# Reading a kernel's input in a second, feature-major layout instead of turning it on TensorE

## The chip, the cores and the metric

The kernel runs on one core of one Trainium2 chip. The metric is the device time of one execution in microseconds (us). The core has five engines that run side by side and meet only at semaphores: TensorE (PE; its weight loads are shown as PEld), VectorE (DVE), ScalarE (ACT), GpSimd (POOL) and SyncE (SP), which here issues all the transfers between the chip's memory (HBM) and the on-chip memory (SBUF). TensorE writes to eight banks of PSUM, 128 partitions of 512 float32 numbers each.

## The reference, cut to what matters

Two model blocks run one after the other over 256 tokens of 1024 features, in float32. The change touches the very first step of the first block: the norm of the input and its product with `w_in`.

```python
def rms_norm(x, g):
    y = xf * lax.rsqrt(jnp.mean(xf * xf, axis=-1, keepdims=True) + EPS)
    return (y * g.astype(jnp.float32)).astype(x.dtype)
...
h = rms_norm(x, norm_mix[l])
z = jnp.einsum('bsd,de->bse', h, w_in[l])
a_x, a_y, b_q, b_f, b_i, b_g, c_q, c_k, c_v = jnp.split(z, split_at, axis=-1)
```

The parts of `z` feed a gated recurrence with a short convolution, a gated linear attention and a softmax attention; then follow an output product, a feed-forward pair, and the second block with its table of experts.

## The kernel before

**Tiles of weights.** Nearly all weights come as a stream of 128x1024 float32 tiles (512 KB each, 432 in all), tile n into slot n mod 4 of `raw`. Each is split into two parts for TensorE: ScalarE copies it rounded into `whi` (function `hi`, line 526, one ACTIVATE), then GpSimd computes the rest `wlo = raw - whi` (function `lo`, line 448, one TENSOR_TENSOR that reads two tensors of SBUF). SyncE may load tile n once `lo` is done with tile n-4; `hi` of tile n also waits until TensorE has used tile n-4. A product of a tile is three matmuls for each 128x128 piece: high by high, low by high, high by low.

**The input.** The activations are split in the same way into `xh` and `xl`, with features on the partitions and the 256 tokens in the free dimension, eight pieces k = 0 to 7 of 128x256. Before, x arrives with tokens on the partitions (`xres`, two transfers, one for each half of the features). TensorE turns it with 16 transposes (line 1066) into banks 0 to 3, two pieces k in each bank, as float32. ScalarE reads a bank and writes `xh` (function `upper`, line 570, gain of the norm as scale). VectorE reads the bank again and writes `xl = bank * gain - xh` (function `turned`, line 1516). TensorE's first tile (`f_tile`, lines 922 to 924) waits for `turned_lo` before every second k. The row of inverse roots of the norm is applied later, when a product is read out of its bank (`in_f`, line 1591): ScalarE sums the squares of x (`sums`, line 545), GpSimd takes the inverse root (`root`, lines 467 and 469), TensorE lays it out as a row in the middle of tile 1 (`mix_row`, line 1117), VectorE copies it to `mix_r` (line 1583).

**The order at the start.** SyncE issues: tile 0, x first half, the identity matrix `ident`, the columns of gains and biases `col`, x second half, tiles 1 to 3, five transfers of constants (all counted by one semaphore, `consts1_in`), then tile 4 and on. ScalarE: `hi(0)`, four pieces of `xh`, `hi(1)`, four pieces of `xh`, two sums of squares, `hi(2)`, `hi(3)`, then two loads of activation tables with a small ACTIVATE after each, `hi(4)` and on. GpSimd: `lo(0)`, `lo(1)`, `root`, `lo(2)`, `lo(3)` and on. TensorE: matmuls on a constant tile (`warm_up`, line 1055), the transposes, then eight tiles with their products in banks 4 and 5 in turn, the small block products of `lru_gates` (line 1077) behind tile 4. Then follows the group `in_M` (lines 964 to 966), in which a tile fills four banks, and between its tiles the scores of the linear attention (line 1108).

Every engine runs its own list in the order in which it is written; a wait holds back all that stands behind it on that engine. TensorE waits for a tile's low part with the first of these lines, and in tile 0 for a pair of pieces of `xl` with the second:

```python
pe.wait_ge(lo_done, count)
pe.wait_ge(S("turned_lo"), turn(turned, 4, k // 2 + 1))
```

Of the kernel before, what the change touches and what calls it, by code (L numbers as in the profile page):

```python
# [53 lines left out]
def acc_freed(group, bank):  # L54
# [4 lines left out]
    if group == "in_M":  # L59
        return (("turned_lo", turn("mix", 4, 1)), ("gy_done", 1), ("ri_done", 1), ("ld_done", 1))[bank]  # L60
# [18 lines left out]
def acc_filled(group, bank):  # L79


    before = GROUPS[:GROUPS.index(group)]
    n = sum(4 if g in TRANSPOSES else 3 for g in before) + bank + 1
    if group == "wout" and bank == 2:
        return n + 2
    return n - 1 if group == "mlp_T" and bank < 2 else n
# [14 lines left out]
F_ORDER = [0, 1, 2, 3, 6, 7, 4, 5, 8, 12, 9, 13, 10, 14, 11, 15]  # L101
Y_BANKS = [0, 1, 4, 5]
# [51 lines left out]
def build(nc, x, stream, ada, cols, rows, lru_w, hgmask, causal, alibi, iota, walr, wup, sguw, keys, out):  # L154
    ctx = ExitStack()
    with ctx:
# [177 lines left out]
        def _(sp):  # L334
# [11 lines left out]
            for n in range(1, R):  # L346
                tile(n, n * P, None)
            sp.dma_start(lw.rearrange("p a b -> p (a b)"), lru_w).then_inc(S("consts1_in"), 16)
            sp.dma_start(msk.rearrange("p a b -> p (a b)").bitcast(U32), hgmask).then_inc(S("consts1_in"), 16)
            sp.dma_start(tmp, rows[:, 0:D].to_broadcast([P, D])).then_inc(S("consts1_in"), 16)  # L350
            sp.dma_start(ali, alibi).then_inc(S("consts1_in"), 16)

            sp.dma_start(gate1, rows[:, 5 * D:6 * D].to_broadcast([P, D])).then_inc(S("gate1_b"), 16)
# [10 lines left out]
            for n in range(R, T_FFN):  # L364
                tile(n % R, n * P, n - R + 1)
                if n in range(T_IN_M, T_IN_M + R):
# [78 lines left out]
        def _(pool):  # L445
# [75 lines left out]
        def _(act):  # L521
# [63 lines left out]

            hi(0, 0, None)
            act.wait_ge(S("col_in"), 16)
            upper("mix_T", c_("mix"), banks=(0, 1))
            hi(1, 0, None)
            upper("mix_T", c_("mix"), banks=(2, 3))  # L590
# [1724 lines left out]
```

## Time and profile before

| | us |
|---|---|
| device time, median of 3 runs | 1384.27 |
| lowest and highest of them | 1382.73, 1386.12 |
| profiled execution, first to last instruction (span) | 1383.7 |
| median of the runs less that span | 0.6 |
| TensorE busy in the span | 1354.1 |
| VectorE, ScalarE, GpSimd busy | 788.2, 713.0, 1056.8 |

The profile is of one execution; the page states its span and no other time of it. How to read it: the timeline lists an engine's instructions in order of time with the start, the duration and, in square brackets, how long the engine sat idle before and what released it. Matmuls overlap, so their durations are longer than the distance between their starts; it is the starts that tell the pace. "PEclk", the granted clock, is 1.00 at TensorE's upper level (2.4 GHz) and 0.50 at the lower (1.2 GHz); in the first microseconds it reads 1.00 although the rows of the warm-up show the slower pace.

### The profile page before, as it was taken

The numbers are of one execution on the slowest core, as the hardware profiler recorded it, in microseconds if no ns is written. First come the engines' busy times: TensorE is split into PE (matmuls) and PEld (weight loads), VectorE is DVE, ScalarE is ACT, GpSimd is POOL, SyncE is SP. The second block draws the span as 40 slices with busy tenths as digits, with TensorE's granted clock in tenths as the row PEclk, the third lists the DMA queues.
The fourth block names the chain that finished last, engine by engine and source line by source line (L and its number), as shares of the span: only waits on it lengthen the run. The fifth ranks groups of instructions, "written<-read, shape, count | busy, mean of one in ns | idle before, by whom it ended". The sixth has DMA issues, their size and how long they took to land.

```text
span 1383.7 us, 27404 instructions
## 1 busy us (share of the span) xinstructions
PE 1354.1 (98%) x9123; PEld 1178.4 (85%) x9123; DVE 788.2 (57%) x1616; ACT 713.0 (52%) x1139; POOL 1056.8 (76%) x466
## 2 busy tenths in 40 slices
PE   8999999999998999999999999999999999999997
PEld 8788999998776887899999988888788888888886
DVE  4755433336159327269990388888877878411113
ACT  7355655555364444435556544444455555566564
POOL 6655788886777786868888877777667777888885
PEclk9999999999999999999999999999999999999999
DMA  8444777774644456745555544454444445565552
GB/s 315 170 169 165 249 282 284 279 257 142 214 148 156 141 178 259 243 138 184 181 183 181 177 164 167 167 167 164 168 140 167 168 166 168 187 236 197 192 189 105
DMA packets 73057, 263.10 MB, mean 190 GB/s; under 512 B 8224, under 2 KB 9120, under 8 KB 72624
## 3 DMA queue, kind: packets, MB, share of 16 engines
q1 hardware_dynamic: 73008, 262.46, 55.0%
q8 instruction: 29, 0.48, 0.1%
q14 instruction: 20, 0.16, 0.0%
HBM read 259.81 MB, written 2.62 MB: 190 GB/s over the span
## 4 chain that ended last, share of the span: by engine, by line
PE 90%; DVE 5%; ACT 2%; issue 1%; DMA 1%; POOL 1%; SPq 0%; POOLq 0%; ACTq 0%; DVEq 0%
PE bank L964 14%; PE bank L965 14%; PE bank L966 14%; PE bank L945 10%; PE bank L922 8%; PE bank L924 8%; PE bank L923 8%; PE bank L946 5%; PE bank L1436 3%; PE bank L949 1%; DVE arena L1956 1%; PE bank L948 1%; PE bank L1108 1%; POOL wlo L448 1%; PE bank L1418 1%
## 5 line engine op out<-in xcount | busy, mean ns | idle before, releaser
L448 POOL TENSOR_TENSOR wlo<-raw,whi 128x1024 fp32r<-128x1024 f32 x432 | 1043.0, 2426 | 293.8 <-ACT whi L526 292.5
L526 ACT ACTIVATE whi<-raw 128x1024 fp32r<-128x1024 f32 x432 | 455.5, 1057 | 337.3 <-PE bank L966 254.2
L964 PE MATMUL bank<-whi,xhl 128*128 128x512 f32 x800 | 320.3, 400 | 12.7 <-DVE arena L1929 5.6
L966 PE MATMUL bank<-whi,xhl 128*128 128x512 f32 x800 | 313.9, 392 | 0.0
L965 PE MATMUL bank<-wlo,xhl 128*128 128x512 f32 x800 | 313.6, 392 | 0.0
L922 PE MATMUL bank<-xhl,whi 128*128 128x256 f32 x896 | 255.0, 285 | 1.9 <-DVE xhl L1516 1.1
L923 PE MATMUL bank<-xhl,whi 128*128 128x256 f32 x896 | 253.5, 283 | 0.0
L924 PE MATMUL bank<-xhl,wlo 128*128 128x256 f32 x896 | 253.4, 283 | 0.0
L945 PE MATMUL bank<-xhl,whi 128*128 128x512 f32 x616 | 222.0, 399 | 1.0 <-DVE xhl L1511 1.0
L964 PEld LDWEIGHTS bank<-whi,xhl 128*128 128x128 f32 x800 | 151.5, 189 | 48.7 <-issue 6.7
L966 PEld LDWEIGHTS bank<-whi,xhl 128*128 128x128 f32 x800 | 151.5, 189 | 32.8
L965 PEld LDWEIGHTS bank<-wlo,xhl 128*128 128x128 f32 x800 | 151.7, 190 | 29.7
L922 PEld LDWEIGHTS bank<-xhl,whi 128*128 128x128 f32 x896 | 171.7, 192 | 5.0 <-DVE xhl L1516 1.3
L923 PEld LDWEIGHTS bank<-xhl,whi 128*128 128x128 f32 x896 | 171.8, 192 | 1.2
L946 PE MATMUL bank<-xhl,wlo 128*128 128x256 f32 x616 | 171.9, 279 | 0.0
L924 PEld LDWEIGHTS bank<-xhl,wlo 128*128 128x128 f32 x896 | 171.7, 192 | 0.0
L2158 DVE TENSOR_TENSOR xhl<-bank,xhl 128x256 fp32r<-128x256 f32 x128 | 53.8, 420 | 148.5 <-ACT bank L878 148.4
L851 ACT ACTIVATE arena<-bank 128x256 f32 x128 | 49.2, 384 | 172.8 <-DVE bank L2168 119.0
L945 PEld LDWEIGHTS bank<-xhl,whi 128*128 128x128 f32 x616 | 115.6, 188 | 25.2 <-DVE xhl L1511 1.3
L2143 DVE TENSOR_TENSOR xs<-bank,xs 128x768 bf16<-128x768 f32 x128 | 121.7, 951 | 0.0
L946 PEld LDWEIGHTS bank<-xhl,wlo 128*128 128x128 f32 x616 | 116.1, 189 | 2.6 <-issue 0.2
L2139 DVE TENSOR_TENSOR bank<-xs,bank 128x256 f32<-128x256 f32 (+1 forms) x128 | 54.4, 425 | 55.2 <-PE bank L1436 53.8
(321 smaller groups left out, 1511.0 us busy)
## 6 DMA issues: line engine op xcount, KB each, us to landing
raw<-stream SPq DMA_DIRECT2D x432, 512.0 KB, 3.3
arena<-ada SPq DMA_DIRECT2D x48, 512.0 KB, 4.9
arena<-rows SPq DMA_DIRECT2D x5, 512.0 KB, 7.6
xs<-x SPq DMA_DIRECT2D x2, 512.0 KB, 6.5
arena<-rows SPq DMA_DIRECT2D x1, 1024.0 KB, 5.7
x_spill<-xs SPq DMA_DIRECT2D x1, 1024.0 KB, 6.3
xs<-x_spill SPq DMA_DIRECT2D x1, 1024.0 KB, 5.5
arena<-hgmask SPq DMA_DIRECT2D x1, 512.0 KB, 8.3
```

The lines of the kernel that those rows point to most:

```text
L448: nc.gpsimd.tensor_tensor(wlo[:, slot, :], raw[:, slot, :], whi[:, slot, :].bitcast(F32), ALU.subtract).then_inc(lo_done, 1)
L526: nc.scalar.activation(whi[:, slot, :], raw[:, slot, :], ACT.Copy).then_inc(hi_done, 1)
L922: nc.tensor.matmul(dst, h_, xh[:, k, :], start=(k == 0), stop=False)
L923: nc.tensor.matmul(dst, h_, xl[:, k, :], start=False, stop=False)
L924: last = nc.tensor.matmul(dst, l_, xh[:, k, :], start=False, stop=(k == KC - 1))
L945: nc.tensor.matmul(dst, h_, xhl[:, :, k, :], start=(k == 0), stop=False)
L946: nc.tensor.matmul(dst[:, 0:T], l_, xh[:, k, :], start=False, stop=False)
L964: nc.tensor.matmul(bank[b][:, :], ah[:, ts], whi[:, slot, cs], start=start, stop=False)
L965: nc.tensor.matmul(bank[b][:, :], ah[:, ts], wlo[:, slot, cs], start=False, stop=False)
L966: last = nc.tensor.matmul(bank[b][:, :], al[:, ts], whi[:, slot, cs], start=False, stop=final)
L2139: ttt(same, bc(0, HALF), counts[:, :, HALF * half:HALF * (half + 1)].to_broadcast([P, 4, HALF]), ALU.is_equal).then_inc(S("same"), 1)
L2143: ttt(oneA[:, slot], same.unsqueeze(1).to_broadcast([P, 3, 4, HALF]), picks[:, 2:5, ts].unsqueeze(3).to_broadcast([P, 3, 4, HALF]), ALU.mu ...
```

## The change

The host hands over x twice: as before (tokens on the partitions, now as two transfers of one token half each), and as `xT`, with features on the partitions, in the layout that `xh` and `xl` have. `xT` is loaded in two halves of 512 KB into the buffer `xg`, which is otherwise used later. ScalarE and VectorE split it from there, so both read SBUF where they read a bank of PSUM. The 16 transposes are gone; four warm-up matmuls that stood between them now stand at the start, 20 in all. The order of the first transfers is new, four of the constants move behind tiles 4, 5 and 6, and `lru_w` gets a semaphore of its own. ScalarE takes `hi(2)` ahead of the sums of squares; GpSimd takes `lo(2)` ahead of `root`. The products of the first tiles go to banks 4, 5, 0, 2, 4, 5, 4, 5; `mix_row` moves from the middle of tile 1 to that of tile 2, and `lru_gates` from behind tile 4 to behind tile 5.

```diff
+F_BANKS = [4, 5, 0, 2, 4, 5, 4, 5]
...
+            xT_all = xg.rearrange("p a b -> p (a b)")
             tile(0, 0, None)
-            x_halves = x.rearrange("p (a d) -> p a d", a=TT)
-            sp.dma_start(xres[:, :, 0:512], x_halves[:, :, 0:512]).then_inc(S("x_in0"), 16)
+            sp.dma_start(col[:, :], cols).then_inc(S("col_in"), 16)
+            x_turned(0)
+            tile(1, P, None)
+            x_turned(1)
+            tile(2, 2 * P, None)
+            x_part(0)
+            x_part(1)
+            tile(3, 3 * P, None)
             sp.dma_start(ident[:, :], iota[:, P:2 * P]).then_inc(S("ident_in"), 16)
-            sp.dma_start(col[:, :], cols).then_inc(S("col_in"), 16)
-            sp.dma_start(xres[:, :, 512:1024], x_halves[:, :, 512:1024]).then_inc(S("x_in1"), 16)
...
-            for n in range(2):
+            for n in range(3):
                 lo(n, n + 1)
             root(S("squares"), squared("mix"), s_(SS["mix"]), rs("mix"), 1.0 / D)
-            for n in range(2, R):
-                lo(n, n + 1)
+            lo(3, R)
...
+            def x_upper(half):
+                act.wait_ge(S(f"xT_in{half}"), 16)
+                for k in range(4 * half, 4 * half + 4):
+                    last = nc.scalar.activation(xh[:, k, :], xg[:, k, :], ACT.Copy, scale=c_("mix", k))
+                    if k % 2:
+                        last.then_inc(S("turned_hi"), 1)
...
-            warm_up(16)
-            pe.wait_ge(S("ident_in"), 16)
-            for b in range(4):
-                if b == 2:
-                    warm_up(4)
-                pe.wait_ge(S(f"x_in{b // 2}"), 16)
-                for tt in range(TT):
-                    for j in range(2):
-                        k = 2 * b + j
-                        last = nc.tensor.transpose(bank[b][:, j * T + tt * P:j * T + (tt + 1) * P],
-                                                   xres[:, tt, k * P:(k + 1) * P], ident[:, :])
-                last.then_inc(acc_ready, 1)
+            warm_up(20)
...
-                if n >= 2:
-                    pe.wait_ge(S("in_f"), n - 1)
-                if n == 1:
+                if n >= R:
+                    pe.wait_ge(S("in_f"), n - 3 if n < 6 else n - 1)
+                if n == 2:
...
-                if n == 4:
+                if n == 5:
                     lru_gates()
...
-            turned("mix", c_("mix"))
+            for b in range(4):
+                v.wait_ge(S("turned_hi"), b + 1)
+                for k in (2 * b, 2 * b + 1):
+                    last = stt(xl[:, k, :], xg[:, k, :], c_("mix", k), xh[:, k, :].bitcast(F32), ALU.mult, ALU.subtract)
+                last.then_inc(S("turned_lo"), 1)
```

SyncE's list from the start of the program, before (the names are the destination and the source of a transfer; `xs` is the buffer of x, `arena` a large buffer in which `xg`, the constants and much else lie):

```order
L338 DMA raw<-stream 128x1024
L342 DMA xs<-x 128x2x512
L343 DMA ident<-iota 128x128
L344 DMA col<-cols 128x108
L345 DMA xs<-x 128x2x512
L338 DMA raw<-stream 128x1024 x3
L348 DMA arena<-lru_w 128x256
L349 DMA arena<-hgmask 128x1024
L350 DMA arena<-rows 128x1024
```

and in the changed kernel:

```order
L339 DMA raw<-stream 128x1024
L349 DMA col<-cols 128x108
L342 DMA arena<-xT 128x1024
L339 DMA raw<-stream 128x1024
L342 DMA arena<-xT 128x1024
L339 DMA raw<-stream 128x1024
L345 DMA xs<-x 128x1024 x2
L339 DMA raw<-stream 128x1024
L357 DMA ident<-iota 128x128
L358 DMA arena<-lru_w 128x256
L339 DMA raw<-stream 128x1024
```

One small transfer instead of two stands ahead of the input, tile 1 stands between the input's halves, and 1 MB more is loaded.

ScalarE's list from its first tile on, before (`whi` is a tile's high part, `xhl` holds `xh` and `xl`):

```order
L526 ACTIVATE whi<-raw 128x1024
L570 ACTIVATE xhl<-bank,col 128x256 x4
L526 ACTIVATE whi<-raw 128x1024
L570 ACTIVATE xhl<-bank,col 128x256 x4
L545 ACTIVATE arena,st<-xs 128x1024 x2
L526 ACTIVATE whi<-raw 128x1024 x2
```

and in the changed kernel:

```order
L537 ACTIVATE whi<-raw 128x1024
L600 ACTIVATE xhl<-arena,col 128x256 x4
L537 ACTIVATE whi<-raw 128x1024
L600 ACTIVATE xhl<-arena,col 128x256 x4
L537 ACTIVATE whi<-raw 128x1024
L556 ACTIVATE arena,st<-xs 128x1024 x2
L537 ACTIVATE whi<-raw 128x1024
```

The source of the eight pieces is now in SBUF, and tile 2's high part has passed the sums of squares.

## Rows read from the trace of the kernel before

**Rows 1.** The page: busy us, share of the span, number of instructions of each engine.
```profile
PE 1354.1 (98%) x9123; PEld 1178.4 (85%) x9123; DVE 788.2 (57%) x1616; ACT 713.0 (52%) x1139; POOL 1056.8 (76%) x466
```

**Rows 2.** Timeline, TensorE, 0 to 19 us; last row: all its waits from 18.9 to 72.5.
```profile
1.06 5.83 PE L1055 MATMUL bank<-arena 128*128 128x128 f32 x32 [1.06 <-POOL arena L473]
...
10.74 0.36 PE L922 MATMUL bank<-xhl,whi 128*128 128x256 f32 x1
...
13.54 0.39 PE L922 MATMUL bank<-xhl,whi 128*128 128x256 f32 x1 [1.13 <-DVE xhl L1516]
...
16.46 0.28 PE L924 MATMUL bank<-xhl,wlo 128*128 128x256 f32 x1
...
18.95 0.35 PE L922 MATMUL bank<-xhl,whi 128*128 128x256 f32 x1 [0.57 <-DVE arena L1591]
...
PE bank L922 <- DVE arena L1591: 0.6, 1, 0.6
```

**Rows 3.** Timeline, SyncE's first issue of x, and both transfers' time to landing.
```profile
1.18 0.66 SPq L342 DMA_DIRECT2D xs<-x  x1
...
DMA to landing us min/median/max: 6.5/6.5/6.6
```

**Rows 4.** Timeline, ScalarE, 0 to 19 us.
```profile
4.08 1.06 ACT L526 ACTIVATE whi<-raw 128x1024 fp32r<-128x1024 f32 x1 [2.07 <-DMA raw<-stream]
8.76 1.57 ACT L570 ACTIVATE xhl<-bank,col 128x256 fp32r<-128x256 f32 x4 [3.63 <-PE bank L1066]
10.79 1.06 ACT L526 ACTIVATE whi<-raw 128x1024 fp32r<-128x1024 f32 x1 [0.46 <-DMA raw<-stream]
...
13.18 1.07 ACT L545 ACTIVATE arena<-xs 128x1024 f32<-128x1024 f32 x1
...
17.29 1.28 ACT L597 ACT_TABLE_LOAD   x1
```

**Rows 5.** Timeline, GpSimd, 5 to 22 us.
```profile
5.28 2.35 POOL L448 TENSOR_TENSOR wlo<-raw,whi 128x1024 fp32r<-128x1024 f32 x1 [4.28 <-ACT whi L526]
11.93 2.38 POOL L448 TENSOR_TENSOR wlo<-raw,whi 128x1024 fp32r<-128x1024 f32 x1 [4.30 <-ACT whi L526]
...
15.74 0.71 POOL L469 TENSOR_TENSOR st<-st 128x2 f32<-128x2 f32 x1
16.42 4.75 POOL L448 TENSOR_TENSOR wlo<-raw,whi 128x1024 fp32r<-128x1024 f32 x2
```

**Rows 6.** Timeline, VectorE, second half of `xl`.
```profile
12.61 1.66 DVE L1516 SCALAR_TENSOR_TENSOR xhl<-bank,col,xhl 128x256 fp32r<-128x256 f32 x4 [1.23 <-ACT xhl L570]
```

**Rows 7.** Timeline, VectorE and GpSimd, 392 to 418 us; last row: L2067 from 655.5 to 656.
```profile
392.44 3.40 DVE L1948 SCALAR_TENSOR_TENSOR arena<-arena,st 128x1024 f32<-128x1024 f32 x1 [2.38 <-POOL st L469]
...
416.59 1.22 DVE L1952 SCALAR_TENSOR_TENSOR arena<-arena 128x1024 f32<-128x1024 f32 x1 [10.74 <-ACT arena L794]
...
392.37 15.73 POOL L448 TENSOR_TENSOR wlo<-raw,whi 128x1024 fp32r<-128x1024 f32 x5
...
L2067 DVE TENSOR_TENSOR arena<-arena x1: 2622/2622/2622, 655.1 to 655.1; 128x256 f32<-128x256 f32 x1
```

**Rows 8.** Timeline, TensorE; then stretches: busy by engine, granted clock, DMA share, GB/s.
```profile
439.61 0.77 PE L964 MATMUL bank<-whi,xhl 128*128 128x512 f32 x1 [5.59 <-DVE arena L1929]
...
441.02 0.63 PE L964 MATMUL bank<-whi,xhl 128*128 128x512 f32 x1
441.45 0.63 PE L965 MATMUL bank<-wlo,xhl 128*128 128x512 f32 x1
...
999.27 0.80 PE L964 MATMUL bank<-whi,xhl 128*128 128x512 f32 x1 [2.64 <-DVE xhl L2158]
...
438.00:439.00 1.00, 0.00 (x0) 0.00 (x0) 1.00 (x2) 0.11 (x1) 0.00 (x0) 0.89 0.54 111
...
445.00:446.00 1.00, 1.00 (x9) 1.00 (x8) 1.00 (x1) 0.90 (x1) 1.00 (x1) 0.70 0.00 0
...
998.00:999.00 1.00, 0.00 (x0) 0.00 (x0) 0.85 (x3) 0.69 (x3) 0.82 (x1) 0.78 0.29 37
```

More of the change, by code:

```diff
@@ L59, in acc_freed @@
     if group == "in_M":
-        return (("turned_lo", turn("mix", 4, 1)), ("gy_done", 1), ("ri_done", 1), ("ld_done", 1))[bank]
+        return (("in_f", 3), ("gy_done", 1), ("ri_done", 1), ("ld_done", 1))[bank]
     if group == "wout":
@@ L82, in acc_filled @@
     before = GROUPS[:GROUPS.index(group)]
-    n = sum(4 if g in TRANSPOSES else 3 for g in before) + bank + 1
+    n = sum(0 if g == "mix_T" else 4 if g in TRANSPOSES else 3 for g in before) + bank + 1
     if group == "wout" and bank == 2:
@@ L151, in sync, with build @@
         self.eng.wait_ge(self.sem, self.n)
-def build(nc, x, stream, ada, cols, rows, lru_w, hgmask, causal, alibi, iota, walr, wup, sguw, keys, out):
+def build(nc, x, xT, stream, ada, cols, rows, lru_w, hgmask, causal, alibi, iota, walr, wup, sguw, keys, out):
     ctx = ExitStack()
@@ L338, in tile, with x_turned, x_part @@
                 sp.dma_start(raw[:, slot, :], stream[bass.ds(row, P), :]).then_inc(raw_full[slot], 16)
-            tile(0, 0, None)
-            x_halves = x.rearrange("p (a d) -> p a d", a=TT)
-            sp.dma_start(xres[:, :, 0:512], x_halves[:, :, 0:512]).then_inc(S("x_in0"), 16)
-            sp.dma_start(ident[:, :], iota[:, P:2 * P]).then_inc(S("ident_in"), 16)
-            sp.dma_start(col[:, :], cols).then_inc(S("col_in"), 16)
-            sp.dma_start(xres[:, :, 512:1024], x_halves[:, :, 512:1024]).then_inc(S("x_in1"), 16)
[L346 to L353, printed above, removed]
+            def x_turned(half):
+                sp.dma_start(xT_all[:, half * D:(half + 1) * D], xT[:, half * D:(half + 1) * D]).then_inc(S(f"xT_in{half}"), 16)
+            def x_part(tt):
+                sp.dma_start(xres[:, tt, :], x[:, tt * D:(tt + 1) * D]).then_inc(S(f"x_in{tt}"), 16)
+            xT_all = xg.rearrange("p a b -> p (a b)")
+            tile(0, 0, None)
+            sp.dma_start(col[:, :], cols).then_inc(S("col_in"), 16)
[6 more added lines that the diff above has]
+            tile(3, 3 * P, None)
+            sp.dma_start(ident[:, :], iota[:, P:2 * P]).then_inc(S("ident_in"), 16)
+            sp.dma_start(lw.rearrange("p a b -> p (a b)"), lru_w).then_inc(S("lru_in"), 16)
             def ada_tile(n, row=None, free=None):
@@ L584, in upper_shifted @@
                             .then_inc(S("turned_hi"), 1)
+            def x_upper(half):
[4 more added lines that the diff above has]
+                        last.then_inc(S("turned_hi"), 1)
             hi(0, 0, None)
             act.wait_ge(S("col_in"), 16)
-            upper("mix_T", c_("mix"), banks=(0, 1))
+            x_upper(0)
             hi(1, 0, None)
-            upper("mix_T", c_("mix"), banks=(2, 3))
-            act.wait_ge(S("x_in0"), 16)
-            act.wait_ge(S("x_in1"), 16)
+            x_upper(1)
+            hi(2, 0, None)
             for tt in range(TT):
+                act.wait_ge(S(f"x_in{tt}"), 16)
                 sums(xres[:, tt, :], tt, D, xn, s_(SS["mix"]), S("squares"))
-            for n in range(2, R):
-                hi(n, 0, None)
+            hi(3, 0, None)
             nc.scalar.activation(sil, c_("c"), ACT.Sigmoid).then_inc(S("sil_sig"), 1)
@@ L1055, in warm_up @@
                     nc.tensor.matmul(bank[5][:, 0:P], ones, ones, start=True, stop=True)
[L1057 to L1068 removed]
+            warm_up(20)
             def lru_gates():
[L1071 removed]
+                pe.wait_ge(S("lru_in"), 16)
+                pe.wait_ge(S("in_f"), 4)
                 pe.wait_ge(S("xc_done"), 1)
@@ L1679, in _ @@
             totals(1)
[L1681 removed]
+            v.wait_ge(S("consts1_in"), 48)
             def level_acc(n):
```

21 lines of the change are left out of this document (14 added, 7 removed).

## The prediction

> **What bounds the kernel now.** I read the page first: TensorE is busy 1354.1 of 1383.7 us [rows 1], so only what moves TensorE counts. Then its timeline at the start. It warms up from 1.06 us, turns x from 8.00, starts tile 0 at 10.74 and idles 1.13 us in the middle of it, waiting for `xl`; it reaches tile 2 at 18.95 after 0.57 us of idle time, and from there to 72.5 us it has no other wait [rows 2]. The reader is to see that all the slack that an edit of the head can win lies before 18.95. The wait at 18.95 is printed against VectorE's `in_f`, but the code needs there only the first `in_f`, done long before, and `lo(2)`: GpSimd ran `lo(2)` and `lo(3)` from 16.42 in 4.75 us, so `lo(2)` ended at 18.8 [rows 5]. My unit is therefore the time at which TensorE begins tile 2, before 18.9. Behind it the same 6 tiles and `lru_gates` follow; only `mix_row` (about 0.25 us) moves from ahead of that point to behind it.
>
> **Transfers.** x's first half, second of the large transfers, was issued at 1.18 and landed 6.5 us later, at 7.7 [rows 3]. Tile 1, the fourth large one, landed at 10.8, where `hi(1)` started [rows 4]: 1.5 us for each 512 KB, small transfers included. In the changed order `xT` takes the second place, tile 1 the third, `xT`'s second half the fourth, tile 2 the fifth. Late bound: the places' old times, 7.9, 9.4, 10.8, 12.3. Early bound: tile 0 landed by 4.08 [rows 4], 0.4 for `col` and an estimated 1.3 for each large one: 5.7, 7.0, 8.3, 9.6. One of the two small transfers stays and the packets are longer, so I take the middle: 6.8, 8.2, 9.5, 10.9; the halves of x 12.2 and 13.5, tile 3 at 14.8. The extra 1 MB costs only this delay of x and tile 3; the moved constants have users after 25 us.
>
> **ScalarE.** Four pieces of `xh` took 1.57 us from PSUM [rows 4]; reading SBUF I take the same. Pieces 0 to 3: 6.8 to 8.4; `hi(1)` (1.06) to 9.4; pieces 4 to 7, 9.5 to 11.1; `hi(2)` to 12.2. Then the sums of squares follow x: until 14.7.
>
> **GpSimd and VectorE, the step that decides.** `lo(1)` follows `hi(1)`: 9.5 to 11.9. `lo(2)` is ready at 12.3. VectorE's `xl` falls just here, and in the changed kernel it reads `xg` and `xh`, both in SBUF. In rows 7 the same operation with two SBUF inputs took 1.22 us at 416.59, while GpSimd had nothing to run, and 3.40 us at 392.44, against `lo`: GpSimd's five `lo` took 15.73 us there in place of 12. A 128x256 operation with two SBUF inputs took 2.62 us at 655.1 [rows 7], where a piece of `xl`, the same size, takes 0.42 (1.66 for four [rows 6]). Read in order of time, the two engines take turns, a whole instruction each, and whoever comes second waits. Before the change it cost nothing: `xl` read PSUM and one SBUF tensor, and its last four pieces took 1.66 us at 12.61, in the middle of `lo(1)` from 11.93 [rows 5, 6].
>
> The Trainium skill, page "SBUF — State Buffer", section "Who interferes with whom", has this as a rule: a VectorE instruction with two SBUF inputs contends with a GpSimd instruction that reads SBUF, one with at most one SBUF input does not. By that rule, with which rows 5 to 7 agree, the sum is the one below; if the place of the inputs made no difference, it would be rival A.
>
> Pieces 0 to 3 of `xl` run from 7.8 (`lo(0)` is over at 7.63 [rows 5]) to 9.5, just before `lo(1)`. Piece 4 could start at 10.4 and waits for `lo(1)` until 11.9, done 12.3. Now `lo(2)` has come and goes first: 12.3 to 14.75. Piece 5 then ends at 15.15, pieces 6 and 7 at 16.8, since the two small instructions of `root` (0.71 us for the second [rows 5]) come between them. `lo` itself is hardly later, and nobody is queued behind it in need: tile 1 has its low part at 11.9.
>
> **TensorE.** 20 warm-ups, 40 records, end at about 7.8 (32 records took 5.83 us from 1.06 on [rows 2], 8 more at the later pace of 0.12 another 1.0). k = 0, 1 at 8.65, k = 2, 3 at 9.5 to 10.2. Then it idles until piece 5 is there, 15.15: 4.9 us. Bounds for what that does to its clock: an idle time of 1.13 us did nothing [rows 2]; one of 5.59 us, before 439.61, and one of 2.64 us, before 999.27, each ended with the granted clock at 0.50: it fell inside 438 to 439 and 998 to 999, that is 5 and 2 us after the last matmul [rows 8]. It rose again in 445 to 446, some 6 us after work had resumed at 439.61. At the lower level matmuls of 512 columns start every 0.43 us [rows 8]; in place of the 0.12 us of these (24 from 13.54 to 16.46 [rows 2]) I take 0.225. In the warm-up it must have risen sooner: 32 records in 5.83 us are, at 0.225 and 0.12 us each, 18 slow ones, an estimate of 4 us of work at the low clock [rows 2]. I take 5 us, between 4 and 6: the clock is low from before 15.15 to 20.15. Pieces 4 and 5 (6 matmuls) end at 16.5, 6 and 7 run 16.8 to 18.15, then tile 1 does 9 matmuls at the low clock and 15 in 1.8 us: tile 2 begins at 21.95.
>
> **The sum.** 21.95 + 0.25 for `mix_row` - 18.9 = +3.3 us. Removed and costed at nothing: the 16 transposes (about 2 us of TensorE) lie ahead of tile 0, where TensorE waits anyway; the gained 2 us at the first matmul (8.65 against 10.74) go into the longer wait. The four banks lift waits on `in_f`, which did not bind: `in_f(0)` comes now after `mix_row`, near 24.5, and tile 4, which needs it, at 28. `lru_gates` behind tile 5 waits for nothing new; ScalarE's `hi(9)` is queued behind it and is done with 3 us to spare. `hi(4)` waits for tile 0 (18.2) and the two table loads from 17.29 on [rows 4], as before, so `lo(4)` at about 22 is in time for tile 4. Behind tile 2 the distance to the old times stays as it is to the end. On its own execution: 1383.7 + 3.3 = 1387.0; the median stood 0.6 above the span, so 1387.6.
>
> **Rivals.**
> A. *The engines do not get in each other's way*, or tile 2 lands so late (after 12.4) that `lo(2)` lets all four pieces pass. Without any turn-taking `xl` ends at 12.1, tile 0 at 12.8, tile 1 at 15.7; then `hi(4)`, behind the table loads, holds tile 4 at 22.2 instead of 24.7: -2.5 us, 1381.8. With only `lo(1)` in the way: about -1.5. For it: the pieces are short. Against it: rows 7. This is what would make the kernel faster than before. 0.12.
> B. *Turn-taking, but the clock stays up*. Then tile 0 ends at 17.5, tile 1 at 20.4: +1.7, 1386.0. For it: 4.9 us lies below the longer of the two rows. Against it: the shorter one, 2.64 us. 0.17.
> C. *Slower than can be overlooked: xT lands at its late bound*. All of ScalarE's chain follows its landing, so 1.1 us are added, and if the clock needs 6 us rather than 5, another 0.4: +4.8, 1389.1. It decides from a landing of 7.6 us on. For it: x's first half landed at 7.7 from a like place [rows 3]. 0.14.
> D. *An early landing helps*. It does not: with `xT` at 6.0, `hi(1)` ends sooner, `lo(1)` starts before piece 3 of `xl` and blocks that one as well; `xl` ends near 16.6 all the same. It is inside the forecast.
>
> **Chances.** Forecast, turn-taking and a fallen clock: 0.52, at 1387.6. A 0.12, B 0.17, C 0.14, others 0.05 (1391 or more, or a gain that I do not see). About 0.3%, 4.1 us here, is what a measurement can tell from no change. The forecast is within it in four cases of five, B and A are within it, C is over it mostly. So faster 0.03, same 0.75, slower 0.22. The range goes from 1384.0 (under B) to 1390.0 (over C); A is left out.
>
> **What would show it.** In the changed profile: `xl` (VectorE, 128x256, eight of them) has two or three members of 2 to 3 us, beginning while `lo(1)` and `lo(2)` run; TensorE has one wait of 3 to 5 us in tile 0 behind VectorE; the granted clock is 0.50 somewhere from 13 to 20 us; tile 2 begins at 21 to 23. `xT`'s first half lands at 5.7 to 7.9. If all eight pieces take 0.4 to 0.5 us, A holds; if the wait is there and the clock reads 1.00, B. The prediction is wrong if the difference arises anywhere behind 40 us, where I expect every wait of the old profile again, shifted.

## The result, and the profile after

The changed kernel takes 1391.43 us (median of 4 runs, 1390.80 to 1393.20); the kernel before took 1383.72 beside it (4 runs). The ratio is 1.0054, with a 95% interval of 1.0041 to 1.0067. The forecast was 1387.6, range 1384.0 to 1390.0, with "slower by over 0.3%" at 0.22. The time lies above the range, and the kernel is slower. The profiled execution took 1390.8 us, with a span of 1388.5. One execution of a kernel below (a_split_warm) took 2705 us in place of some 1384 and is left out of its figures.

The head went much as forecast. Timelines of the changed kernel, 0 to 19 us: ScalarE, GpSimd, VectorE, TensorE (start, busy us, engine, line, operation, idle time ahead and what ended it):

```profile
6.96 1.70 ACT L600 ACTIVATE xhl<-arena,col 128x256 fp32r<-128x256 f32 x4 [1.68 <-DMA arena<-xT]
8.57 1.04 ACT L537 ACTIVATE whi<-raw 128x1024 fp32r<-128x1024 f32 x1
...
9.69 2.38 POOL L460 TENSOR_TENSOR wlo<-raw,whi 128x1024 fp32r<-128x1024 f32 x1 [1.92 <-ACT whi L537]
12.32 2.64 POOL L460 TENSOR_TENSOR wlo<-raw,whi 128x1024 fp32r<-128x1024 f32 x1 [0.26 <-ACT whi L537]
...
7.98 1.67 DVE L1592 SCALAR_TENSOR_TENSOR xhl<-arena,col,xhl 128x256 fp32r<-128x256 f32 x4 [7.98 <-ACT xhl L600]
10.54 5.11 DVE L1592 SCALAR_TENSOR_TENSOR xhl<-arena,col,xhl 128x256 fp32r<-128x256 f32 x4 [0.88 <-ACT xhl L600]
...
12.80 0.39 PE L939 MATMUL bank<-xhl,whi 128*128 128x256 f32 x1 [2.11 <-DVE xhl L1592]
15.70 0.58 PE L939 MATMUL bank<-xhl,whi 128*128 128x256 f32 x1 [1.92 <-DVE xhl L1592]
...
20.68 0.28 PE L939 MATMUL bank<-xhl,whi 128*128 128x256 f32 x1
```

These answer to [rows 2, 4 to 6]. The first four pieces of `xl`, with GpSimd idle, took 1.67 us; the last four, beside `lo(1)` and `lo(2)`, took 5.11, and GpSimd's second `lo` 2.64 in place of 2.35. TensorE waited twice for VectorE inside tile 0, and tile 2 begins at 20.68 (18.95 before).

TensorE's busy time and granted clock (the column behind the count) by stretch, in the head and then twice behind it, changed kernel (0.50 is the lower of the two levels, 1.2 GHz):

```profile
15.00:16.00 1.00, 0.30 (x1) 0.62 1.01 401
16.00:17.00 1.00, 1.00 (x6) 0.50 1.03 410
17.00:18.00 1.00, 1.00 (x7) 0.50 1.03 414
18.00:19.00 1.00, 1.00 (x7) 0.67 1.03 410
...
323.00:340.00 17.00, 17.00 (x90) 0.80 0.26 90
...
524.00:535.00 11.00, 9.31 (x40) 0.84 0.65 256
```

and of the kernel before:

```profile
323.00:340.00 17.00, 16.68 (x109) 1.00 0.18 63
...
524.00:535.00 11.00, 11.00 (x52) 1.00 0.60 232
```

The clock fell in the head, as forecast. It also fell at 329.3 us, for 6.8 us, and at 527.2, for 3.4: two falls that the trace of before does not have. (A fall and its length are worked out from the granted clock of stretches of 4 us: 4 us at 0.82, for instance, hold 1.44 us at the lower of the two levels; or they are read off the clock record in the trace.) The falls of [rows 8], before 439.6 and before 999.3, are there in both; the second is half as long in the changed kernel (3.4 us against 6.8).

The waits of TensorE of over 1 us from 323 to 1010 us, of the changed kernel and then of the kernel before, in us in total, times, longest:

```profile
PE bank L981 <- DVE arena L1942: 5.6, 1, 5.6
PE bank L981 <- POOL wlo L460: 2.7, 6, 0.8
PE bank L981 <- DVE xhl L2171: 2.6, 1, 2.6
PE bank L1058 <- DVE arena L2036: 1.4, 1, 1.4
PE bank L981 <- DVE xhl L1520: 1.3, 1, 1.3
```
```profile
PE bank L964 <- DVE arena L1929: 5.6, 1, 5.6
PE bank L964 <- POOL wlo L448: 2.7, 6, 0.8
PE bank L964 <- DVE xhl L2158: 2.6, 1, 2.6
PE bank L964 <- DVE xhl L1511: 1.6, 1, 1.6
```

No new wait explains a loss. The first product of the first `m_tile` (a tile of the group `in_M`) starts 1.9 us later than before; changed kernel, then before:

```profile
40.22 0.40 PE L981 MATMUL bank<-whi,xhl 128*128 128x512 f32 x1
```
```profile
38.35 0.40 PE L964 MATMUL bank<-whi,xhl 128*128 128x512 f32 x1
```

The first product behind the transposes of the second input part starts at 338.6 (333.4), +5.2. So 2 us arise in the head and 3 at one place where the program is unchanged and TensorE waits for nobody. The spans differ by 4.8 us, but that is no proof that nothing else happened: matmul by matmul the distance is +4.8 from 340 us on, +4.1 behind 446, +5.8 behind the fall at 527, +6.3 from 600 us on, and +4.8 again behind 1010, where the old kernel has the longer fall.

### The profile page after: what moved, and what is told of

Read it like the earlier page. It is cut to its first block, busy times and chain, and to the rows that moved or that the text cites. A ratio compares the mean times of both kernels' runs of the same rounds, so it can differ in the third digit from the quotient of the medians.

```text
span 1388.5 us, 27371 instructions
## 1 busy us (share of the span) xinstructions
PE 1356.2 (98%) x9107; PEld 1180.3 (85%) x9107; DVE 792.2 (57%) x1616; ACT 713.2 (51%) x1139; POOL 1057.7 (76%) x466
## 4 chain that ended last, share of the span: by engine, by line
PE 89%; DVE 5%; ACT 2%; issue 2%; DMA 1%; POOL 1%; SPq 0%; POOLq 0%; ACTq 0%; DVEq 0%
PE bank L981 14%; PE bank L983 13%; PE bank L982 13%; PE bank L962 10%; PE bank L939 8%; PE bank L941 8%; PE bank L940 8%; PE bank L963 5%; PE bank L1445 3%; PE bank L966 1%; DVE arena L1969 1%; POOL wlo L460 1%; PE bank L965 1%; PE bank L1116 1%; PE bank L1427 1%
```

## The experiments

All times are medians; "first m_tile" is the first start of line 981 or what answers to it, in the one profiled execution. The "clock" is the mean granted clock of each run's span.

| kernel | us | ratio to before (95%) | clock of the runs | first m_tile |
|---|---|---|---|---|
| before | 1383.7 to 1384.4 | | 0.992 to 0.996 | 38.3 |
| changed | 1391.43 | 1.0054 (1.0041, 1.0067) | 0.989 to 0.991 | 40.2 |
| a_repeat (the changed kernel again) | 1390.92 | 1.0046 (1.0031, 1.0061) | 0.990 to 0.992 | 42.2 |
| a_lo_waits | 1386.70 | 1.0013 (1.0002, 1.0024) | 0.990 to 0.996 | 38.4 |
| b_later | 1385.82 | 1.0010 (1.0001, 1.0018) | 0.994 to 0.996 | 39.9 |
| b_xT_bound | 1384.27 | 1.0000 (0.9991, 1.0009) | 0.993 to 0.996 | 37.5 |
| a_pad7 | 1390.38 | 1.0045 (1.0032, 1.0058) | 0.992 to 0.995 | 44.2 |
| a_pad14 | 1394.13 | 1.0079 (1.0066, 1.0091) | 0.989 to 0.992 | 44.8 |
| a_warm | 1389.23 | 1.0047 (1.0032, 1.0061) | 0.990 to 0.995 | 43.5 |
| a_split | 1384.59 | 1.0002 (0.9993, 1.0011) | 0.992 to 0.996 | 38.6 |
| a_keep | 1388.85 | 1.0035 (1.0022, 1.0047) | 0.994 to 0.995 | 43.0 |
| b_keep | 1384.40 | 1.0004 (0.9995, 1.0013) | 0.995 to 0.996 | 37.7 |
| a_split_warm | 1384.71 | 1.0003 (0.9993, 1.0013) | 0.993 to 0.996 | 37.6 |
| a_warm_one | 1388.01 | 1.0023 (1.0011, 1.0036) | 0.993 to 0.996 | 40.7 |

Names that begin with a are edits of the changed kernel, with b of the kernel before. The ratio goes over all runs of a row and is not exactly that of the two medians. Of the kernel before, 29 runs taken together had spans from 1379.0 to 1384.8, mean 1382.5; the eight of the changed kernel and its repetition lay at 1388.5 to 1390.9, mean 1389.3. The time is about 1.8 to 2.3 us above its own span in the runs of all kernels. The rows were measured at different times, each against runs of the kernel before beside it; those medians lie up to 0.7 us apart, and differences between rows carry that too. (One run of the kernel before, of 1383.49 us, reads a clock of 0.945; it is not in the range of the table.)

The questions came in this order. Is the head's loss the turn-taking and the clock, as forecast? Do the falls behind the head come from what the change moves or adds ("moved work"), from all work coming later, from luck, or from the fall in the head itself, which sets TensorE's place for what follows ("locked")? What does each part weigh?

**a_repeat**: the changed kernel without an edit.

> The changed kernel once more, for a second profile of it. Theory F (the granted clock falls at places that depend on when a stretch comes, and it comes at the same time in every execution): tile 2 begins at 20.6 us, the clock is 0.50 again from about 329 and from about 527 us, span about 1388.5 to 1391. Rival L (each execution draws its own places by luck): the falls stand elsewhere, and the span differs by 3 us or more from 1388.5. Both: 1391 us, 7 us above the kernel before.

Timelines of ScalarE, VectorE and TensorE:

```profile
8.73 1.70 ACT L600 ACTIVATE xhl<-arena,col 128x256 fp32r<-128x256 f32 x4 [3.50 <-DMA arena<-xT]
...
12.22 5.21 DVE L1592 SCALAR_TENSOR_TENSOR xhl<-arena,col,xhl 128x256 fp32r<-128x256 f32 x4 [0.79 <-ACT xhl L600]
...
16.69 0.39 PE L939 MATMUL bank<-xhl,whi 128*128 128x256 f32 x1 [4.23 <-DVE xhl L1592]
```

`xT` landed at 8.7 us here, not at 6.9; `xl` ends at 17.4, TensorE has one wait of 4.2 us, tile 2 begins at 22.6 and the first `m_tile` comes at 42.2. The clock falls again near 329 us (at 331.4, for 6.8 us), but not near 527, and the span is 1389.4. So theory F had the span and one of the two falls; rival L's span, 3 us or more away, did not come. In this and the eight later profiles that load `xT` as the change does, ScalarE starts on it between 8.2 and 9.1 us: the profile of the changed kernel is the exception.

**a_lo_waits**: GpSimd starts `lo(1)` only when `xl` is complete.

```diff
             for n in range(3):
+                if n == 1:
+                    pool.wait_ge(S("turned_lo"), 4)
                 lo(n, n + 1)
```

> The changed kernel, but GpSimd starts the low part of tile 1 only when all eight pieces of the input's low part are written, so VectorE and GpSimd never want SBUF at once there. Theory T (turn-taking costs the head its time): VectorE's last four pieces take 1.7 us instead of 5.1, TensorE's waits of 2.1 and 1.9 us in tile 0 shrink to one below 0.3, the clock stays at 1.00 up to 25 us, tile 1 begins at about 14.9 behind its own low part, tile 2 at about 17.8 instead of 20.6, so 2.8 us sooner there. Rival R (reading the second operand from SBUF is slow in itself): the last four pieces still take near 5 us and tile 2 begins later than 20.6. Of the end of the program theory T alone says nothing, since the falls of the clock further back may come or go: 1386 to 1390 us.

Timelines of VectorE and GpSimd:

```profile
11.67 1.68 DVE L1594 SCALAR_TENSOR_TENSOR xhl<-arena,col,xhl 128x256 fp32r<-128x256 f32 x4 [0.79 <-ACT xhl L602]
13.43 4.73 POOL L460 TENSOR_TENSOR wlo<-raw,whi 128x1024 fp32r<-128x1024 f32 x2 [5.76 <-ACT whi L539]
```

Apart from each other the pieces of `xl` took 1.68 us again and each `lo` 2.37. The first `m_tile` stands at 38.4, as before the change, though the clock fell in this head too (at 10.9 us, behind a wait of 3.05), which the expectation did not have; tile 2 begins at 18.8 and not at 17.8. The turn-taking is real, and most of the head's loss. Its median is still 1.0013 times before, with an interval that just excludes no change; in its profile, the slowest of its ten runs, the loss arises behind 325 us, and the clocks of its runs spread from 0.990 to 0.996.

**b_later**: the kernel before with 13 more warm-up matmuls, so that everything comes later but nothing is moved.

```diff
-            warm_up(16)
+            warm_up(29)
```

> The kernel before with 13 more warm-up matmuls at its start, nothing else: all that follows comes about 2.1 us later, as in the changed kernel behind its head. Theory F (the place in time decides where the clock falls): the clock falls near 329 us and near 527 us as in the changed kernel, the span grows by about 4.8 us, the time by 5. Rival O (the losses behind the head are the changed kernel's own, by its banks or its transfers): no fall at 329 or 527, and the time grows by 2.1 us and no more.

The profile stays 1.3 to 1.6 us behind the old one up to 999 us, with no fall near 329 us; there it lacks the fall that the old profile has and ends 1.4 us ahead of it. Coming 1.5 us later does not by itself bring the falls.

**b_xT_bound**: the kernel before, with the changed kernel's extra input of 1 MB, of which it reads 16 columns.

```diff
+            sp.dma_start(probe[:, :], xT[:, 0:16]).then_inc(S("probe_in"), 16)
```

> The kernel before with the feature-major copy of x as one more input of 1 MB, of which only 16 columns are read, in the middle of the program. Theory I (one more input costs time outside the span of the instructions): the time grows by about 2 us while the span stays at 1383.7, within 0.5. Rival N (it costs nothing): the time stays within 0.5 us of the kernel before, and the 2 us more between time and span of the changed kernel have another cause.

The time is that of before, to 0.1%: the input as such costs nothing. But its profile has a fall at 325.7 us, low for 6.8, with +3.0 us behind it. TensorE's work is that of the kernel before, so that kernel, too, can meet this fall, it seems in some of its executions. That turned the question: not what makes the clock fall there, but why the changed kernel seems to meet it each time.

**a_pad7, a_pad14**: seven, or fourteen, matmuls of ones behind tile 2, where TensorE waits for nothing until 40 us.

```diff
+                if n == 2:
+                    for _ in range(7):
+                        nc.tensor.matmul(bank[3][:, 0:P], ones, ones, start=True, stop=True)
```

> The changed kernel with seven more warm-up matmuls (ones times ones, into a bank that nobody reads before the gates), put behind TensorE's tile 2. TensorE waits for nothing between tile 2 and the first m_tile, so everything behind it comes later by the seven, an estimated 1.5 to 1.9 us. Theory 'locked': in the changed kernel the clock falls in the head in every execution, and TensorE's work then always stands at the same distance behind the rise that ends that fall; this distance is what makes it meet a fall near 329 us (2.8 us) and mostly one near 527 us (1.5 us) each time. Moved on by 1.5 to 1.9 us TensorE is at another distance, and at least the fall near 329 us is gone: more work, less time, about 1391.4 + 1.7 - 2.8 - 1.5 = 1388.8, range 1387.6 to 1390.5. Rival 'moved work': the falls and stalls behind the head come from what the change reorders (loads, banks, gates), so seven more matmuls only cost their own time: 1391.4 + 1.7 = 1393.1, range 1392.5 to 1394, with the fall near 329 us as in the changed kernel. Rival 'chance': the fall near 329 us comes in some executions and not in others, whatever the distance: spans differ by over 3 us within this kernel.

> The same with fourteen warm-up matmuls, an estimated 3.0 to 3.8 us, about as much as one low stretch of the clock lasts in the trace of the changed kernel (3.36 us). Theory 'locked': at that distance the old alignment comes back, with the falls near 329 us and 527 us: 1391.4 + 3.4 = 1394.8, range 1393.8 to 1396, so the second seven cost over 4 us while the first seven save. Rival 'moved work': each seven costs the same, 1394.8 here and 1393.1 for seven. Rival 'chance': spans differ by over 3 us within this kernel and its mean is 1394.8 less some share of 4.3. This run tells nothing alone between the first two; the step from seven to fourteen does.

The filler in TensorE's timeline, and then the stretch around 329 us, with seven:

```profile
26.22 1.72 PE L1142 MATMUL bank<-arena 128*128 128x128 f32 x14
```
```profile
323.00:340.00 17.00, 17.00 (x108) 1.00 0.38 123
```

and with fourteen:

```profile
25.23 3.29 PE L1142 MATMUL bank<-arena 128*128 128x128 f32 x28
```
```profile
323.00:340.00 17.00, 17.00 (x95) 0.83 0.38 127
```

Each seven take 1.6 us. The first seven cost nothing in time (1390.38, against 1391.43 and 1390.92 without them), the second seven 3.75 us. In the profiles the fall near 329 us is gone with seven and back with fourteen. This is what "locked" said, within its ranges, and "moved work" is refuted: it wanted 1393.1 with seven. "Chance" is not refuted for fourteen: its spans run from 1389.6 to 1394.7, so the alignment is not rigid there.

**a_warm**: warm-ups in two places of tile 0.

```diff
-            warm_up(20)
+            warm_up(23)
...
+                    if turned == "mix" and k in (4, 6):
+                        warm_up(6)
```

> The changed kernel with three more warm-up matmuls ahead of tile 0 and six in each of its two waits (before pieces 5,6 and before 7,8 of xl), so that TensorE is busy where it idled. VectorE's pieces still take turns with GpSimd's lo(1) and lo(2), but the clock should not fall in the head. By my forecast the turn-taking alone costs 1.7 us of the 3.3 and the clock 1.6: the first m_tile at some 39.0 to 39.6 us instead of 40.2. Theory 'locked' says that with the fall in the head the fixed distance goes too: the falls near 329 and 527 us come in some executions only, spans spread over 3 us or more as they do before the change, and the median is 1391.4 - 1.3 in the head - about 2 behind it = 1388, range 1386.5 to 1389.3. Rival 'moved work': the 3.6 us behind the head stay: 1391.4 - 1.3 = 1390.1, range 1389.5 to 1391, with the narrow spread of the changed kernel.

Timeline of TensorE, the product after the wait and the warm-ups behind it:

```profile
16.59 0.38 PE L941 MATMUL bank<-xhl,whi 128*128 128x256 f32 x1 [2.89 <-DVE xhl L1594]
...
17.40 2.71 PE L1074 MATMUL bank<-arena 128*128 128x128 f32 x12
```

The edit was aimed at the waits of one profile. With `xT` landing later there is one wait, before the third pair of pieces; six warm-ups filled less than half of it, the clock fell at 17.5 us all the same, and the other six stood in the way, 2.7 us at the low clock. The first `m_tile` came at 43.5 in place of the expected 39.0 to 39.6: a miss, and inconclusive.

**a_split**: VectorE makes `lo(1)` itself between the fourth and the fifth piece, and GpSimd takes `lo(2)` when `xl` is complete.

```diff
-            for n in range(3):
-                lo(n, n + 1)
+            lo(0, 1)
+            pool.wait_ge(S("turned_lo"), 4)
+            lo(2, 3)
...
+                if b == 1:
+                    v.wait_ge(lo_done, 1)
+                    v.wait_ge(hi_done, 2)
+                    nc.vector.tensor_tensor(wlo[:, 1, :], raw[:, 1, :], whi[:, 1, :].bitcast(F32),
+                                            ALU.subtract).then_inc(lo_done, 1)
```

with `warm_up(23)` at the start and `warm_up(2)` ahead of k = 4.

> The changed kernel with both costs of the head taken away: VectorE makes lo(1) itself between the fourth and the fifth piece of xl, GpSimd waits for the last piece before lo(2), so that no piece of VectorE runs beside a piece of GpSimd (only lo(0) may still lie beside the first ones), and TensorE gets three more warm-ups ahead of tile 0 and two in its wait. By the durations of the traces: pieces 1 to 4 end about 9.7 to 11.0, lo(1) 1.2 us behind, pieces 5 to 8 by 12.6 to 14.0, lo(2) 2.4 us behind that; tile 0 done 13.5 to 14.9, tile 2 begins 16.5 to 18 where it began at 18.9 before the change and at 20.6 after it. No fall of the clock in the head. Then the first m_tile at 36 to 37.5 us (38.3 before the change). Theory 'locked' (the 3.6 us behind the head come only from the fixed distance that the fall in the head sets): 1384.2 - 1 to 2.5 = 1381.7 to 1383.2, spread as before the change. Rival 'moved work': 3.6 us more than that, 1385.3 to 1386.8.

All that the change moves behind the head (loads, banks, gates) is in this kernel, and it takes the time of before: 1384.59 beside 1384.16, below the 1385.3 of "moved work". But it gains nothing: the first `m_tile` is at 38.6, not at 36 to 37.5, since `xT` landed at 9.1 and the clock fell at 12.2 (the expectation below for a_split_warm has 12.56).

**a_keep, b_keep**: denser work at the place of the fall near 329 us, in either kernel.

```diff
             for g in range(2, 6):
                 ada_columns(g)
-                keep_warm(2, bank[6][:, :])
+                keep_warm(4, bank[6][:, :])
```

> The changed kernel with four instead of two keep-warm matmuls behind each of the four groups of eight one-column products that stand behind the first feed-forward part (324 to 333 us; two of these matmuls stand 0.55 us from start to next start there). So it does 4 times 0.5 = 2.0 us more work, at the place where the clock falls at 329.28 us in its trace and stays low for 6.8 us, which costs 2.8. Theory: the changed kernel meets this fall in nearly every execution, and denser work there takes it away: 1391.4 + 2.0 - 2.8 = 1390.6, range 1389.8 to 1391.6, and a profile with clock 1.0 from 323 to 340 us. Rival: the fall there is rare in the changed kernel, or comes all the same: the time grows by the full 2.0, 1393.4 or more.

> The kernel before with the same edit, 2.0 us more work. Theory: it meets the fall near 329 us in few executions (the profiled one has none), so there is little to save: 1384.2 + 2.0 - (0 to 1) = 1385.2 to 1386.2, and what the edit costs here is 1.8 to 2.8 us more than what it costs in the changed kernel; that difference is what this one place adds to the 7 us of the change. Rival: the fall comes as often before the change as after it; then the edit costs the same in both kernels, within 0.7 us.

Timeline of one group, and the granted clock of the stretch, changed kernel with the edit:

```profile
328.42 0.95 PE L1149 MATMUL bank<-st,arena 128*128 128x1 f32 x8
329.23 1.19 PE L1066 MATMUL bank<-uh 128*128 128x512 f32 x4
```
```profile
323.00:340.00 17.00, 17.00 (x103) 1.00 0.37 123
```

The added work is 1.9 us (four times 0.48). The changed kernel got 2.1 to 2.6 us *faster* by it, the kernel before 0.35 slower; in mean spans -2.4 and +0.9. So the edit saves 2.4 to 3.3 us more in the changed kernel than before the change, where 1.8 to 2.8 were expected. Both medians lie below their expected ranges, by 0.95 and 0.8 us. All six runs of a_keep have a clock of 0.994 or 0.995. The profile of a_keep has no fall near 527 us either, which may be the excess; this was not tested apart.

**a_split_warm**: a_split with `warm_up(31)` and `warm_up(4)`.

> The kernel in which VectorE makes lo(1) and no piece of xl runs beside GpSimd (1384.59, first m_tile at 38.6 us, its clock still fell at 12.56 us after TensorE had idled for 2.7 us), now with 31 instead of 23 warm-up matmuls ahead of tile 0 and four instead of two in its wait, so that TensorE idles nowhere in the head as long as xT lands by 8.5 to 9 us. Theory: the low stretch of 3.44 us goes and gives back up to half of it, 1.3 to 1.7 us: first m_tile at 36.9 to 37.4 us, 1384.6 - 1.5 = 1383.1, range 1382.2 to 1384.2. Rival: the warm-ups stand in the way of pieces that are there earlier and cost what they save: 1384.2 to 1385.4; or the clock falls all the same: 1384.6 or more.

Timelines of VectorE and TensorE:

```profile
11.35 1.23 DVE L1600 TENSOR_TENSOR wlo<-raw,whi 128x1024 fp32r<-128x1024 f32 x1
12.49 1.67 DVE L1595 SCALAR_TENSOR_TENSOR xhl<-arena,col,xhl 128x256 fp32r<-128x256 f32 x4
...
13.43 0.39 PE L942 MATMUL bank<-xhl,whi 128*128 128x256 f32 x1 [0.21 <-DVE xhl L1595]
```

No fall in the head, no wait over 0.3 us in it, first `m_tile` at 37.6: the head does what it should, 1.0 us sooner than a_split's. The median, 1384.71, does not show it, and the clocks of its runs are no higher than a_split's. So neither version beats the kernel before; the expected 1383.1 was missed. Its profiled execution had the fall near 329 us.

**a_warm_one**: the wait filled where it is.

```diff
-            warm_up(20)
+            warm_up(28)
...
+                    if turned == "mix" and k == 4:
+                        warm_up(15)
```

> The changed kernel once more with its waits in the head filled, as the traces since taken show them: when xT lands at 8.2 to 8.7 us there is one wait of 4.2 us before pieces 5 and 6 of xl and none before 7 and 8. Eight more warm-up matmuls ahead of tile 0 (28), fifteen in that one wait, none behind it. VectorE's pieces still take turns with GpSimd; only TensorE's clock in the head is spared. If no clock falls in the head, the first m_tile comes at 40.5 to 41.3 us (xl still ends at about 17.2), 1.4 to 1.7 us earlier than in the executions of the changed kernel in which xT landed so late (42.2). Theory 'locked': without the fall in the head the distance that meets the fall near 329 us is no longer set, so the clocks spread as before the change (0.993 to 0.996) and the time is 1391.2 - 1.5 in the head - 1 to 2.5 behind it: 1387.2 to 1388.7. Rival 'the head alone': 1389.4 to 1390, all clocks at 0.990 to 0.992. Rival 'the clock falls in the head all the same, since TensorE's warm-ups are too thin': 1390.5 or more.

Timelines of TensorE and VectorE, and TensorE's clock in the stretch behind the wait:

```profile
12.23 3.51 PE L1074 MATMUL bank<-arena 128*128 128x128 f32 x30
16.64 0.38 PE L941 MATMUL bank<-xhl,whi 128*128 128x256 f32 x1 [0.90 <-DVE xhl L1594]
...
12.15 5.23 DVE L1594 SCALAR_TENSOR_TENSOR xhl<-arena,col,xhl 128x256 fp32r<-128x256 f32 x4 [0.79 <-ACT xhl L600]
```
```profile
16.00:18.00 2.00, 1.36 (x10) 1.00 1.05 409
```

The turn-taking is all there (5.23 us), TensorE still gets its pieces at 16.6, only the clock in the head is spared. The first `m_tile` comes at 40.7 and the median is 1388.01, both inside what "locked" expected, and all seven clocks are at 0.993 to 0.996. Filling one wait with work that nobody uses gives 3 us back, by medians, 1.5 of them in the head and about as much behind it. Not at the fall near 329 us, as far as the two profiles tell: a_warm_one has that fall as a_repeat has it. The distance between the two grows by 0.9 us from 530 to 600 us and by 1.6 near 1005, where a_repeat's clock falls and a_warm_one's does not.

## Where the 7 us are

Three pairs of kernels price the parts, each by first `m_tile` where `xT` landed alike, and by median:

- **Turn-taking of VectorE and GpSimd, about 3 us.** a_warm_one (with it) against a_split_warm (without), neither with a fall in the head: 40.7 against 37.6, 1388.0 against 1384.7.
- **The clock in the head, 1.5 us, and what follows from it behind the head, 1.4.** a_repeat (1390.9; 42.2) against a_warm_one (1388.0; 40.7): `xT` landed at 8.7 in both.
- **The rest, 0.3 to 0.7 us**: a_split_warm against before. Its ratio's interval contains no change.

Together 6.5 to 6.9 us, where a_repeat lost 6.7; since the pairs form one chain of medians from a_repeat down to before, they must add up to about that, and it confirms nothing. The share behind the head comes out larger by the other pair, a_keep against b_keep: about 3 us. I take it as between 1.4 and 3. The head's share depends on the profile of before that it is set against: its first `m_tile` came at 38.3 us, but with the same head at 37.5 in b_xT_bound and at 37.7 in b_keep. Against these a_repeat lost 4.5 to 4.7 us in the head, and 2 or so are left for what lies behind.

What goes with the falls behind the head is an alignment. The table sets the distance from the rise of the clock that ends the fall in the head to the first `m_tile` against what the clock did near 329 us, for the eight profiles with a fall in the head. (a_keep has the edit at that place.)

| kernel | low in the head, us | rise, us | distance, us | fall near 329 us |
|---|---|---|---|---|
| a_repeat | 3.4 | 20.8 | 21.4 | yes |
| changed | 3.4 | 18.7 | 21.6 | yes |
| a_pad7 | 10.2 | 21.7 | 22.5 | no |
| a_split | 3.4 | 15.6 | 23.0 | no |
| a_warm | 3.4 | 20.9 | 22.6 | no |
| a_lo_waits | 3.4 | 14.3 | 24.1 | yes |
| a_pad14 | 3.4 | 20.1 | 24.7 | yes |
| a_keep | 6.8 | 22.5 | 20.5 | no, edited |

The fall near 329 us goes with distances of 21.4, 21.6, 24.1 and 24.7 us, and is missing at 22.5 to 23.0. It does not go with the time: in the changed kernel and its repetition, whose rises lie 2.1 us apart, the fall near 329 us came 310.6 us behind the rise, both times. Without the added matmuls (1.6 and 3.3 us), a_pad7 and a_pad14 stand at 20.9 and 21.4. So all five profiles with the head of the changed kernel have 20.5 to 21.6.

The 310.6 us are no property of the fall in the head, however. The clock records of the traces begin with the rise in the warm-up, at 5.00 us in the changed kernel, 7.13 in a_repeat, 4.02 in a_lo_waits and 5.90 in a_warm_one. In all four the fall near 329 us comes 324.27 us behind that first rise, and a_warm_one has no fall in its head. In b_xT_bound and a_split_warm, again without a fall in the head, it comes 320.85 us behind it, in a_pad14 327.68. So this fall keeps its distance to the clock's own first rise with or without a fall in the head, and what decides is, as far as these profiles tell, where TensorE's work stands against that. A kernel that does not fall in the head meets the fall near 329 us in some executions only: of the profiles without a fall in the head, b_xT_bound, a_split_warm and a_warm_one have it, before and b_later do not.

Why the changed kernel's work stands at so nearly the same distance each time is not shown. One would like to say that TensorE waits for VectorE across the fall and then works the low stretch off, which would tie its place to the rise. That is so in the changed kernel and in a_keep, where work resumed 0.5 and 0.7 us behind the fall, and in a_pad7, which waits inside its longer low stretch; in a_repeat and a_pad14 work had resumed 0.7 and 0.4 us before it. And a fall in the head does not fix the time by itself: a_lo_waits, a_warm and a_split have one each, and their spans run over 5.4 to 5.6 us.

Shown: that denser work at the one place takes the fall away and gains more in the changed kernel than in the one before (a_keep, b_keep), and that the time does not grow when TensorE's work is moved on by 1.6 us (a_pad7), which rules out "moved work". Shown by the clocks of the runs: with the wait in the head filled (a_warm_one) less low clock is met, 0.993 to 0.996 against 0.989 to 0.992. Whether the missing fall in the head does that, or only that all work stands at another place, is not separated. Inferred, since only one execution of each kernel is profiled: that the changed kernel meets the fall near 329 us in every execution; the clocks of its eight runs and its narrow spans, 2.4 us from lowest to highest, speak for it. Open: what spreads the spans of a_pad14 over 5 us, which share the fall near 527 us has, and the exact split between head and rest.

## The prediction, step by step

- **Turn-taking: right.** The last four pieces took 5.11 to 5.23 us in every head with `lo` beside them and 1.67 to 1.68 in those without. `xl` was forecast to end at 16.8; it ended at 15.6 in the first profile and between 17.0 and 17.4 in the others that keep the turn-taking. [Rows 7] had shown it. The rule of the Trainium skill, page "SBUF — State Buffer", section "Who interferes with whom", which the prediction cites, holds in this head: 1.66 us for four pieces with one SBUF input [rows 6] beside `lo(1)`, 5.2 with two. Rival A, which left the turn-taking out, is refuted.
- **The clock in the head: right.** Low from 15.2 for 3.4 us (forecast: from before 15.15, 5 us), and from 17.4 for 3.4 in a_repeat. It cost 1.5 us in the head; the working had 1.6 (the forecast less rival B). That the prices agree although the stretch was a third shorter is in part luck.
- **Landing of `xT`: too early.** 6.8 was taken, with 7.9 as late bound; the first profile had 6.9, the other nine lay over the bound, at 8.2 to 9.1. The interval of 1.3 to 1.5 us for each large transfer was read off transfers that come later. From 4 to 5 us the transfers moved 299 GB/s in the changed kernel's profile, 86 in a_split's and 90 in a_warm's. x's first half landed at 7.7 [rows 3] with the same bytes ahead of it, which should have been the middle, not nearly the bound. The head's +3.3 us became +1.9 (early landing) and +3.8 (late), or up to +4.7 against the earlier heads of b_xT_bound and b_keep.
- **The gain without turn-taking: too large.** Rival A had -2.5 us; a_split_warm, which has neither the turn-taking nor the fall, stands at -0.7 in the head, and within 0.1 us of those of b_xT_bound and b_keep. Taking out the 16 transposes saved nothing: with `xT` at 8.6 the first product comes at 10.65, where it came at 10.74 before (9.88 and 10.12 in those two).
- **"Behind tile 2 the distance to the old times stays as it is to the end": wrong, and the step that failed.** I had named it as what would refute the forecast. It holds for the waits, and for b_later up to 999 us. It does not hold for the clock: I used [rows 8] to price a fall, and took for granted that the falls behind the head are the same ones after the change. The term that stood at nothing was +3 us at one place in the profile, and 1.4 to 3 us by medians.
- **The base: wrong, without harm.** "The median stood 0.6 above the span" set the median of several runs against the span of one. The time is 1.8 us or more above its own span; the profiled execution of before was a long one, with 1383.7 where 29 others have a mean of 1382.5. By the right base the forecast would be 1382.5 + 1.8 + 3.3 = 1387.6 all the same.

The range failed since all its cases were cases of the head. The spread of before was in the times shown, 3.4 us in three runs, for a program that waits at fixed places; asking what differs between those runs would have led to the clock.

## What to carry to other kernels

Before an operand is moved from PSUM to SBUF, look at what GpSimd runs beside its reader: here four small pieces went from 1.7 to 5.2 us, and the transposes that went in exchange had cost nothing that TensorE did not wait for anyway. Where TensorE must wait, matmuls that nobody uses are cheap against a fall of the clock, if they sit in the wait that is really there; take its place from several profiles, since a transfer at the start can land 2 us apart. And when a forecast says "all the rest is only shifted", compare the spread of the runs before with the effect: if executions of one program differ by as much as the effect, something behind the change may depend on where it falls.

## What was not expected of the hardware

- The fall near 329 us came 324.27 us behind the first rise of the clock, in the warm-up, in four profiles, three with a fall in the head in between and one without. And 1.6 us of useless work in between made the kernel no slower.
- TensorE's trace shows it busy without a gap from 323 to 340 us, with a fall inside: groups of eight products of one column (0.95 us each) with two matmuls of 512 columns between. With four in place of two the granted clock read 1.00; but so it did with two in the kernel before, whose profile does not meet the fall.
- The same program on the same chip differed by 5.8 us in its span (1379.0 to 1384.8), with clocks of 0.996 at the low end and 0.993 at the high one.
- ScalarE read the pieces from SBUF in 1.70 us, where four pieces from PSUM took 1.57 [rows 4].
